# Neighbourhood attention on tokens ordered by columns, 208 keys to a half, with the probabilities as the standing operand; and two edits to the order of banks and of the sums of squares

## The chip, the cores and the metric

The kernel runs on one core of a Trainium2 chip. The time is device microseconds of that core, the median of three runs. The core's engines work side by side, each through its own list of instructions in order, and wait for one another on semaphores: TensorE (PE, with its weight loads as PEld), VectorE (DVE), ScalarE (ACT), GpSimd (POOL) and SyncE (SP), which here issues most of the DMAs. PE writes to eight banks of PSUM.

## The reference, cut to what matters

A block of two token mixers and an MLP, then two more layers, on 16 meta tokens and 256 tokens laid out on a grid of 4 rows by 64 columns, width 1024, all in float32. The part that the change rewrites is the neighbourhood attention (8 heads of 64):

```
q, k, v = split(rms_norm(h) @ w_in)                 # h: 16 meta + 256 tokens
for each token at (row r, column c):
    window: all 4 rows, 16 columns from start = clip(c - 8, 0, 48)
    s_win  = q.k * 64**-0.5 + rpb[dr + 7, clip(dc, -15, 15) + 15]   # -1e30 outside the window
    s_meta = q.k_meta * 64**-0.5
    p = softmax(concat(s_win, s_meta))
    o = p_win @ v_win + p_meta @ v_meta
```

A token of columns 0 to 31 never sees a column past 47, and one of columns 32 to 63 never one before 16. Other parts touched are sums of squares over 1024 channels, `rsqrt(mean(x * x))`, for three of the norms: the one ahead of the MLP, the final norm of the first block ("fin") and the norm of the gated linear attention's output ("go").

## The kernel before

Every weight matrix is streamed as units of 128 x 1024 floats (512 KB): SP loads a unit into one of 6 slots of `raw`, ACT rounds it to fp32r (`wh`), DVE takes the rest (`wl = raw - wh`), and PE multiplies three times, `Xh*wl`, `Xh*wh`, `Xl*wh`, with the activations split in the same way. A unit of 256 columns is 24 products, and one of 512 columns (a `rows` unit, where tokens stand as weights and come out as rows) is 6 products to a block of tokens. ACT runs 4 units ahead (`LEAD`), DVE 3 (`AHEAD`), and five buffers hold `wh` and `wl`.

All five engines run through the same list of stages (`Walk.tiles`, `Walk.rows`): after a unit each engine takes one or more `step()`s of a side program, a Python generator with a `yield` at each step, so that the side work of a stage (attention, recurrence, pooling) sits between units. `w.steps` says how many yields go with a unit. After the last unit of a tile an engine runs `leave`, which reads the bank, and a step. In `tiles` the step comes before `leave`, and in `rows` too. Banks 0 to 3 (`main`) are handed out in turn to the matrix products, 4 to 7 (`side`) to side work; `take` waits for the events that freed a bank, and for a group of tiles all banks are taken before its first product.

The first stages are k, q, v, zf, zb, qh (all of `w_in`). k and q are products with unnormed activations `XU`, scaled afterwards by the row `rsB` of 1/rms; v and all later ones use the normed `XA`, which the side program `scaled` makes during k. Attention is the side program from v on. One of its rounds `s` holds, for tokens 0 to 127 and 128 to 255 apart (`t`), the scores of head `s` (`bank<-kT,qT`, 272 keys), the turning of the probabilities of head `s-1` (`bank<-C,sP`, three transposes) and the product with V of head `s-2` (`bank<-PT,vN` and `bank<-PTm,vM`: V's 64 columns stand as weights and 256 queries stream). Between them DVE adds the bias and finds the maximum, ACT takes the exponential with its sum, DVE the reciprocal (`share`), POOL multiplies the probabilities by it (`sP<-sP,nm`), and ACT copies the turned ones. Ordinary float32 products, as these are, show as two instructions each in the trace; a transpose shows as one.

Sums of squares: ACT squares tile after tile, POOL adds those of tiles 1 to 5 to tile 0's, and PE multiplies what is left by a matrix of ones (`bank<-sq,C`), once for the sum of 0 to 5 and once each for 6 and 7.

Of the kernel before, what the change touches and what calls it, by code (L numbers as in the profile page):

```python
# [7 lines left out]
F32 = mybir.dt.float32  # L8
# [22 lines left out]
for _n, _w in [("ident", 128), ("ones", 128), ("negones", 128), ("neguc", 128), ("strict", 128), ("negsb", 128),  # L31
               ("m64", 64), ("negwin", 64), ("cinv", 64), ("tril", 128)]:
    CCOLS[_n] = (sum(w for _, w in CCOLS.values()), _w)
# [67 lines left out]
def flat(x):  # L101
# [12 lines left out]
          "attention_dve": ("most", "score", "score_grid", "share"),  # L114
# [113 lines left out]
class Walk:  # L228
# [40 lines left out]
    def rows(self, label, name, c0, c1, start, unit, leave):  # L269
        width = min(512, c1 - c0)  # L270
        kn = 1024 // width
        for col in range(c0, c1, width):
# [8 lines left out]
            self.step()  # L281
            leave(col - c0)
            self.left.add((label, col - c0))

# [33 lines left out]
def build(nc, ws, par, cst, msk, xt, biasd, late, bsd, wtd, crd, out):  # L318
# [4 lines left out]
    with ExitStack() as ctx:  # L323
# [54 lines left out]
        bias = sbt(pna, "bias", [128, 8, 384])  # L378
        qT = sbt(pna, "qT", [128, 4, 256])
        kT = sbt(pna, "kT", [128, 4, 272])  # L380
        vN = sbt(pna, "vN", [128, 2, 512])
        vM = sbt(pna, "vM", [16, 512])
        sP = [sbt(pna, f"sP{i}", [128, 272]) for i in range(4)]
        PT = [sbt(pna, f"PT{i}", [128, 2, 256]) for i in range(2)]
        PTm = [sbt(pna, f"PTm{i}", [16, 256]) for i in range(2)]
        nmr = [sbt(pna, f"nm{i}", [128, 3]) for i in range(4)]
# [18 lines left out]
        B1s = [sbt(ph2, f"B1{n}", [128, 2112], F32R) for n in "hl"]  # L405

# [65 lines left out]
        ALONE = ("k", "zf", "a", "qk", "glr")  # L472
# [29 lines left out]
        one = {n: sem("l_" + n) for n in ("cst", "par", "crow", "bias", "msk", "wT", "bS", "late", "out")}  # L502
# [47 lines left out]


# [16 lines left out]
        def sync_program(e):  # L568
            c.start("sp")
            e.dma_start(P[:, :], par).then_inc(one["par"], 16)  # L570
            for i in range(len(items)):
                for n in {0: (0,), 1: (1, 2), 2: (3,)}.get(i, ()):
                    e.dma_start(h[:, 2 * n:2 * n + 2, :], xt[:, 2 * n:2 * n + 2, :]).then_inc(x_sem[n], 16)
# [20 lines left out]
        def tensor_program(e):  # L594
# [105 lines left out]
            def t_rows(label, name, c0, c1, X, ready, freed, tokens):  # L700
# [5 lines left out]
                def unit(j, q, kn, width, col):  # L706
                    e.wait_ge(*low_at(j))
                    hi, lo = (x.rearrange("p (k n) -> p k n", n=width) for x in half(j))
                    for b, t in enumerate(tokens):
                        for k in range(kn):  # L710
                            for event in ready(q + k):
                                e.wait_ge(*at(*event))
                            last = q + k == 7
                            m = three(bk(label, col, b)[:, 0:width],
                                      (X[0][:, q + k, t:t + 128], X[1][:, q + k, t:t + 128]),
# [56 lines left out]
            w.side.append(scaled(4))  # L772
            t_tiles("k", "w_in", 512, 1024, (XUh, XUl), unnormed("mix"), lambda t: [("kT", t)], n1=272)
            t_tiles("q", "w_in", 0, 512, (XUh, XUl), unnormed("mix"), lambda t: [("qT", t)], n0=16, n1=272)

            def attention():
                for s in range(10):
                    if s < 8:
                        po = 64 * (s % 2)
                        for t in range(2):  # L780
                            ps = side.take("qk", s, t)
                            e.wait_ge(*at("qT", s // 2))
                            e.wait_ge(*at("kT", s // 2))
                            e.matmul(ps[:, 0:272], qT[po:po + 64, s // 2, 128 * t:128 * t + 128],
                                     kT[po:po + 64, s // 2, :], start=True, stop=True).then_inc(*up("qk", (s, t)))
                            side.give(("qk", s, t), ("score", (s, t)))
                            yield
                    if 1 <= s <= 8:
                        for t in range(2):
                            ps = side.take("turn", s - 1, t)  # L790
                            S = sP[(2 * (s - 1) + t) % 4]
                            e.wait_ge(*at("prob", (s - 1, t)))
                            e.wait_ge(one["cst"], 16)
                            for r in range(2):
                                e.transpose(ps[:, 128 * r:128 * r + 128], S[:, 16 + 128 * r:144 + 128 * r],
# [1959 lines left out]
```

## Time and profile before

| | us |
|---|---|
| median of three runs | 880.95 (878.87 to 882.58) |
| the profiled execution | 878.87 |
| its span | 877.1 |
| PE busy | 843.7 |
| DVE busy | 631.2 |
| ACT busy | 492.1 |
| POOL busy | 112.1 |

The stretches of the program in the span: k and q from 8 to 37 us, v to 58, zf, zb and qh with attention to 128, the recurrence and the other products of `w_in` to 229, the mixing and the MLP to 456, then the second layer (with "fin" near 505) and the third (with "go" from 683 to 715).

A row of the timeline gives start and duration of an instruction or of a merged run of like ones. PE's instructions are pipelined, so that their durations overlap; what one costs is read from its start to the start of the next. In brackets stands how long the engine had been idle and who is inferred to have released it.

### The profile page before, as it was taken

What the parts mean: (1) busy time and instruction counts of PE and PEld (TensorE: products, weight loads), DVE (VectorE), ACT (ScalarE), POOL (GpSimd) and SP (SyncE); (2) the same over time, 40 slices, a digit from 0 to 9 for tenths busy, and PEclk for the clock granted to TensorE, in tenths of its full rate; (3) what the DMA queues carried; (4) which work ended last, traced back from release to release, by engine and by line L of the source; (5) the groups of instructions that cost most, each with busy time, mean ns of one, the idle gap of its engine ahead of it and who ended that gap; (6) DMA issues with size and microseconds to landing.
All of it is one profiled execution on the core that took longest, in us unless ns stands there. A gap on an engine that the chain in (4) does not pass through costs nothing.

```text
span 877.1 us, 16387 instructions
## 1 busy us (share of the span) xinstructions
PE 843.7 (96%) x6574; PEld 799.0 (91%) x6574; DVE 631.2 (72%) x1045; ACT 492.1 (56%) x884; POOL 112.1 (13%) x129
## 2 busy tenths in 40 slices
PE   5989989999999999999999899999999999999996
PEld 5967768998899999999999799999997999999995
DVE  6855636995699887878799776776788549455573
ACT  6544435775556747474666653554577457566541
POOL 0021227530102000000030420000202020000001
PEclk9999999999999999999999999999999999999999
DMA  9632334445458998989878445555656336545431
GB/s 359 243 106 68 97 97 129 128 149 150 116 195 273 317 354 303 364 295 367 277 246 286 162 149 181 172 193 193 192 158 191 108 96 198 187 144 155 144 112 48
DMA packets 47098, 168.93 MB, mean 193 GB/s; under 512 B 5168, under 2 KB 6320, under 8 KB 46896
## 3 DMA queue, kind: packets, MB, share of 16 engines
q1 hardware_dynamic: 46592, 165.34, 56.7%
q10 hardware_dynamic: 432, 2.56, 0.7%
q8 instruction: 52, 0.85, 0.4%
q14 instruction: 22, 0.18, 0.1%
HBM read 166.83 MB, written 1.05 MB: 191 GB/s over the span
## 4 chain that ended last, share of the span: by engine, by line
PE 82%; DVE 10%; ACT 4%; issue 2%; DMA 1%; POOL 1%; SPq 0%; POOLq 0%; DVEq 0%; ACTq 0%
PE bank L183 81%; DVE wl L222 4%; DVE raw L210 1%; ACT wh L192 1%; PE bank L186 1%; DMA raw<-in_ws 1%; DVE B1l L210 1%; DVE h L210 1%; ACT sq L189 1%; DVE B0l L222 0%; ACT B1h L189 0%; ACT L198 0%; DVE A L210 0%; ACT th L189 0%; POOL sq L222 0%
## 5 line engine op out<-in xcount | busy, mean ns | idle before, releaser
L222 DVE TENSOR_TENSOR wl<-raw,wh 128x1024 fp32r<-128x1024 f32 x259 | 323.8, 1262 | 19.7 <-ACT wh L192 19.0
L192 ACT CAST wh<-raw 128x1024 fp32r<-128x1024 f32 x259 | 269.2, 1047 | 111.4 <-PE bank L183 56.0
L183 PE MATMUL bank<-XAh,wl 128*128 128x256 f32 (+1 forms) x896 | 257.4, 287 | 5.1 <-DVE wl L222 4.5
L183 PE MATMUL bank<-XAh,wh 128*128 128x256 f32 (+1 forms) x896 | 251.2, 280 | 0.0
L183 PE MATMUL bank<-XAl,wh 128*128 128x256 f32 (+1 forms) x896 | 251.1, 280 | 0.0
L183 PEld LDWEIGHTS bank<-XAh,wl 128*128 128x128 f32 x896 | 170.5, 190 | 9.6 <-issue 6.3
L183 PEld LDWEIGHTS bank<-XAh,wh 128*128 128x128 f32 x896 | 170.8, 191 | 0.2
L183 PEld LDWEIGHTS bank<-XAl,wh 128*128 128x128 f32 x896 | 170.8, 191 | 0.0
L183 PE MATMUL bank<-B1h,wl 128*128 128x256 f32 (+1 forms) x464 | 130.2, 281 | 2.4 <-DVE B1l L210 2.4
L183 PE MATMUL bank<-B1h,wh 128*128 128x256 f32 (+1 forms) x464 | 129.0, 278 | 0.0
L183 PE MATMUL bank<-B1l,wh 128*128 128x256 f32 (+1 forms) x464 | 129.0, 278 | 0.0
L183 PE MATMUL bank<-B0h,wl 128*128 128x256 f32 (+1 forms) x392 | 110.8, 283 | 1.2 <-DVE B0l L222 1.2
L183 PE MATMUL bank<-B0h,wh 128*128 128x256 f32 (+1 forms) x392 | 109.3, 279 | 0.0
L183 PE MATMUL bank<-B0l,wh 128*128 128x256 f32 (+1 forms) x392 | 109.2, 279 | 0.0
L183 PEld LDWEIGHTS bank<-B1h,wl 128*128 128x128 f32 x464 | 87.2, 188 | 2.9 <-ACT B1h L189 2.8
L222 POOL TENSOR_TENSOR sq<-sq 128x256 f32<-128x256 f32 x25 | 29.7, 1187 | 470.5 <-ACT sq L189 468.9
L183 PEld LDWEIGHTS bank<-B1l,wh 128*128 128x128 f32 x464 | 87.6, 189 | 0.0
L183 PEld LDWEIGHTS bank<-B1h,wh 128*128 128x128 f32 x464 | 87.3, 188 | 0.1
L183 PEld LDWEIGHTS bank<-B0h,wl 128*128 128x128 f32 x392 | 73.9, 188 | 2.1 <-issue 2.0
L183 PEld LDWEIGHTS bank<-B0l,wh 128*128 128x128 f32 x392 | 74.0, 189 | 0.0
L183 PEld LDWEIGHTS bank<-B0h,wh 128*128 128x128 f32 x392 | 73.8, 188 | 0.1
L183 PE MATMUL bank<-wl,XAh 128*128 128x512 f32 (+1 forms) x176 | 62.9, 358 | 0.0
(247 smaller groups left out, 1219.3 us busy)
## 6 DMA issues: line engine op xcount, KB each, us to landing
raw<-in_ws SPq DMA_DIRECT2D x307, 512.0 KB, 4.5
bias<-in_bias ACTq DMA_DIRECT2D x1, 1536.0 KB, 9.4
h<-in_xt SPq DMA_DIRECT2D x4, 272.0 KB, 4.8
out<-h SPq DMA_DIRECT2D x4, 256.0 KB, 2.2
C<-in_cst SPq DMA_DIRECT2D x1, 544.0 KB, 7.7
crow<-in_crow ACTq DMA_DIRECT2D x1, 512.0 KB, 12.9
wT<-in_wt SPq DMA_DIRECT2D x1, 512.0 KB, 5.9
bS<-in_bs SPq DMA_DIRECT2D x1, 512.0 KB, 6.7
```

What stands on the lines that cost most here:

```text
L183: return self.real.matmul(*a, **k)
L186: return self.real.transpose(*a, **k)
L189: return self.real.activation(*a, **k)
L192: return self.real.copy(*a, **k)
L210: return self.real.scalar_tensor_tensor(*a, **k)
L222: return self.real.tensor_tensor(*a, **k)
```

## The change

**Order of the tokens.** A second copy of the input, `in_xk`, holds the 256 tokens by groups of eight columns, in each group row by row, with the 16 meta tokens in the middle: tokens 0 to 127 (columns 0 to 31), meta, tokens 128 to 255. It is loaded as `hK` in place of `h` at the start, and k, q and v are all made from it, unnormed; V's rows are scaled by `rcol`, the column of 1/rms, which three small products turn out of `rsK`. The keys of a half lie side by side: 208 of them for queries of columns 0 to 31 (128 tokens, 16 meta, 64 tokens), and 208 for the others. `in_xt` is loaded into `h` later, by ACT's queue, and `XA` is made during q instead of k; POOL puts `rsK` into the old order (`rsB`).

**Attention.** Both halves of a head go through one step. Scores are two products of 208 columns into one bank; bias and mask are added for 416 columns at once, meta keys included. The probabilities are turned without being divided first, by four transposes (keys 0 to 127 of one half, 128 to 255 of the other, and 112 keys around the meta tokens for each). They then stand as weights and V streams, 64 columns at a time: four products per head, out by queries. DVE divides the result of two heads (`oN`), two transposes per pair of heads turn it back, and ACT and DVE write it to `B0h` and `B0l` in the old order. POOL's multiplication is gone.

**Order of banks.** `Walk.rows` runs `leave` before the last step. Each tile of q takes a bank of its own.

**Sums.** All eight squares of the MLP's norm are added by POOL, and one product is taken, later. For "fin", ACT squares six tiles after the first half of the stage vn and two after the second, where it was four and four, and POOL adds tiles 1 to 5 after the first half. For "go", POOL adds the two squares of a head, and one product per head is left of two, one unit later.

```diff
@@ Walk.rows
                 if q + kn < 8:
                     self.step()
-            self.step()
             leave(col - c0)
             self.left.add((label, col - c0))
+            self.step()
...
-        ALONE = ("k", "zf", "a", "qk", "glr")
+        ALONE = ("k", "q", "zf", "a", "qk", "glr")
...
@@ tensor_program
-            w.side.append(scaled(4))
-            t_tiles("k", "w_in", 512, 1024, (XUh, XUl), unnormed("mix"), lambda t: [("kT", t)], n1=272)
-            t_tiles("q", "w_in", 0, 512, (XUh, XUl), unnormed("mix"), lambda t: [("qT", t)], n0=16, n1=272)
+            w.side.append(scaled(8))
+            XU = (XUh, XUl)
+            t_tiles("k", "w_in", 512, 1024, XU, unnormed("mix"), lambda t: [("kT", t)], n1=272)
+            t_tiles("q", "w_in", 0, 512, XU, unnormed("mix"), lambda t: [("qT", t)], n1=272)
...
+                        ps = side.take("scores", s)
+                        e.wait_ge(*at("qT", s // 2))
+                        e.wait_ge(*at("kT", s // 2))
+                        for b in range(2):
+                            m = e.matmul(ps[:, 208 * b:208 * b + 208], qT[po:po + 64, s // 2, b, :],
+                                         kT[po:po + 64, s // 2, 64 * b:64 * b + 208], start=True, stop=True)
+                        m.then_inc(*up("scores", s))
...
+                        e.transpose(ps[:, 0:128], S[:, 0:128], cst_("ident"))
+                        e.transpose(ps[:, 128:256], S[:, 288:416], cst_("ident"))
+                        e.transpose(ps[0:112, 256:384], S[:, 64:176], cst_("ident"))
+                        e.transpose(ps[0:112, 384:512], S[:, 208:320], cst_("ident")).then_inc(*up("turn", s - 1))
...
+                        for b in range(2):
+                            o = bk("pv", hh // 2)[:, 128 * b + 64 * (hh % 2):128 * b + 64 * (hh % 2) + 64]
+                            z = slice(0, 80) if b else slice(64, 112)
+                            e.matmul(o, PT[hh % 2][:, 128 * b:128 * b + 128], vN[:, b, vs], start=True, stop=False)
+                            m = e.matmul(o, PTm[hh % 2][z, 128 * b:128 * b + 128], vM[z, vs], start=False, stop=True)
+                        m.then_inc(*up("pv", hh))
...
+                        ps = side.take("na_turn", p)
+                        e.wait_ge(*at("out_nat", p))
+                        for b in range(2):
+                            m = e.transpose(ps[:, 128 * b:128 * b + 128], oN[p % 2][:, 128 * b:128 * b + 128],
+                                            cst_("ident"))
...
+            ps = side.take("rcol")
+            e.wait_ge(*at("rs", "mix"))
+            for b, t in enumerate((0, 144, 64)):
+                m = e.matmul(ps[:, 2 * b:2 * b + 2], rsK[:, t:t + 128], cst_("ident", 2), start=True, stop=True)
...
+            t_rows("v", "w_in", 1024, 1536, XU, unnormed("mix"), lambda b, col: [("v", (col, b))],
+                   ((0, 128), (144, 272), (64, 176)))
...
-            square_sums("mlp", ("o", 7), ("rs", "mlp"))
+            def mlp_sum():
+
+                if ("up0", 1) in w.left and sums:
+                    sums.clear()
+                    ps = side.take("sums", "mlp")
+                    e.wait_ge(*at("sq_add", ("mlp", 7)))
+                    e.matmul(ps[:, 0:256], cst_("ones"), sq_of("mlp", 0)[:, 0:256], start=True, stop=True).then_inc(
...
@@ scalar_program
             e.dma_start(bias[:, :, :], biasd).then_inc(one["bias"], 16)
+            e.dma_start(negw[:, :], negwd).then_inc(one["negw"], 16)
+            e.dma_start(h[:, :, :], xt).then_inc(one["h"], 16)
             e.dma_start(crow[:, :], crd).then_inc(one["crow"], 16)
...
-                for t in range(col // 128, col // 128 + 4):
+                for t in (6, 7) if col else range(6):
                     square("fin", t, ("h_down", t))
...
@@ vector_program
+                    e.wait_ge(*at("rs_nat", 0))
+                    e.wait_ge(one["h"], 16)
                     e.scalar_tensor_tensor(v[:, :], h[:, k, :], par_("norm_mix", k), rsB[:, :], ALU.mult,
...
+                        e.tensor_tensor(S[:, :], ps[:, 0:416], bias[:, s, :], ALU.add).then_inc(*up("score", s))
+                        e.wait_ge(*now("score"))
+                        e.tensor_reduce(nm[:, 0:2], S[:, :].rearrange("p (b n) -> p b n", b=2), AX.X, ALU.max,
...
@@ gpsimd_program
+                    a, b = (sq_of("go", (hh, v))[:, 0:256] for v in range(2))
+                    e.wait_ge(*at("go_sq", (hh, 1)))
+                    e.tensor_tensor(a, a, b, ALU.add).then_inc(*up("go_add", hh))
```

**What stands in a row on the engines.** First PE, in the stage zb, between two units (`XA*, w*`): before, the six transposes of a head's probabilities and its three products with V.

```order
L183 MATMUL bank<-XAl,wh 128x256
L186 MATMUL bank<-C,sP 128x128 x2
L186 MATMUL bank<-C,sP 16x128
L186 MATMUL bank<-C,sP 128x128 x2
L186 MATMUL bank<-C,sP 16x128
L183 MATMUL bank<-PT,vN 64x256 x2
L183 MATMUL bank<-PTm,vM 64x256
L183 MATMUL bank<-XAh,wl 128x256
```

And now: four transposes and four products of 64 columns.

```order
L183 MATMUL bank<-XAl,wh 128x256
L186 MATMUL bank<-C,sP 128x128 x2
L186 MATMUL bank<-C,sP 112x128 x2
L183 MATMUL bank<-vN,PT 128x64
L183 MATMUL bank<-vM,PTm 128x64
L183 MATMUL bank<-vN,PT 128x64
L183 MATMUL bank<-vM,PTm 128x64
L183 MATMUL bank<-XAh,wl 128x256
```

Second ACT, at the end of the stage v (`vM`, `vN`: the copies that free v's banks; `sP,nm`: the exponentials of a head). Before, the copies stand behind the exponentials.

```order
L192 CAST wh<-raw 128x1024
L189 ACTIVATE sP,nm<-sP,nm 128x272 x2
L192 COPY vM<-bank 16x512
L192 COPY vN<-bank 128x512 x2
L192 CAST wh<-raw 128x1024
```

Now they stand ahead of them, and the rows of V are scaled on the way.

```order
L192 CAST wh<-raw 128x1024
L195 ACTIVATE vN<-bank,rcol 128x512 x2
L195 ACTIVATE vM<-bank,rcol 112x512
L189 ACTIVATE sP,nm<-sP,nm 128x208 x2
L192 CAST wh<-raw 128x1024
```

Third DVE, between the scaling of k's second pair of tiles (`kT`) and that of q's (`qT`): before, all of `XAl<-vt,XAh` was over by then.

```order
L222 TENSOR_TENSOR kT<-bank,rsB 128x272 x2
L222 TENSOR_TENSOR wl<-raw,wh 128x1024 x2
L210 SCALAR_TENSOR_TENSOR qT<-bank,rsB 128x256 x2
L222 TENSOR_TENSOR wl<-raw,wh 128x1024 x2
L210 SCALAR_TENSOR_TENSOR qT<-bank,rsB 128x256 x2
```

Now the making of `XA` from `h` begins behind `kT`; these are the first rows of it (five more tiles of `vt` and six of `XAl` follow ahead of the second `qT`).

```order
L222 TENSOR_TENSOR kT<-bank,rsK 128x272 x2
L222 TENSOR_TENSOR wl<-raw,wh 128x1024
L210 SCALAR_TENSOR_TENSOR vt<-h,P,rsB 128x272 x2
L222 TENSOR_TENSOR XAl<-vt,XAh 128x272
L222 TENSOR_TENSOR wl<-raw,wh 128x1024
L210 SCALAR_TENSOR_TENSOR vt<-h,P,rsB 128x272
L222 TENSOR_TENSOR XAl<-vt,XAh 128x272
```


## Rows read from the trace of the kernel before

**Rows 1.** The page: busy engines, and the granted clock in 40 slices.

```profile
PE 843.7 (96%) x6574; PEld 799.0 (91%) x6574; DVE 631.2 (72%) x1045; ACT 492.1 (56%) x884; POOL 112.1 (13%) x129
...
PEclk9999999999999999999999999999999999999999
```

**Rows 2.** Waits of PE for POOL's multiplication: us in total, times, longest.

```profile
PE bank L186 <- POOL sP L219: 4.0, 3, 2.5
```

**Rows 3.** Timeline of PE and ACT at the end of v: start, duration.

```profile
57.31 1.18 PE L183 MATMUL bank<-kT,qT 64*128 64x272 f32 x4
...
61.49 0.37 PE L183 MATMUL bank<-XAh,wl 128*128 128x272 f32 x1 [3.00 <-DVE wl L222]
...
60.68 0.56 ACT L192 COPY vM<-bank 16x512 f32<-16x512 f32 x1
```

**Rows 4.** Timeline of PE, parts of attention between units.

```profile
66.12 0.82 PE L186 MATMUL bank<-C,sP 128*128 128x128 f32 x6
...
66.86 1.08 PE L183 MATMUL bank<-PT,vN 128*64 128x256 f32 x4
...
67.87 0.64 PE L183 MATMUL bank<-PTm,vM 16*64 16x256 f32 x2
...
68.44 0.39 PE L183 MATMUL bank<-XAh,wl 128*128 128x272 f32 x1
...
71.67 1.18 PE L183 MATMUL bank<-kT,qT 64*128 64x272 f32 x4
...
72.78 0.44 PE L186 MATMUL bank<-C,sP 128*128 128x128 f32 x2
```

**Rows 5.** Timeline of PE in the third layer: small products.

```profile
705.72 1.02 PE L183 MATMUL bank<-sq,C 128*128 128x256 f32 x4
...
706.67 0.45 PE L183 MATMUL bank<-gq,KI 128*64 128x64 f32 x8
...
706.95 0.40 PE L183 MATMUL bank<-gq,gk 128*64 128x64 f32 x4
...
707.28 0.66 PE L183 MATMUL bank<-gq,K 128*128 128x64 f32 x4
...
707.75 0.36 PE L183 MATMUL bank<-XAh,wl 128*128 128x256 f32 x1
...
711.88 0.37 PE L183 MATMUL bank<-XAh,wl 128*128 128x256 f32 x1
...
714.70 0.38 PE L183 MATMUL bank<-sq,C 128*128 128x256 f32 x1
```

**Rows 6.** Timeline of PE near 505 us; POOL's additions of squares.

```profile
505.29 0.45 PE L183 MATMUL bank<-sq,C 128*128 128x256 f32 x1 [3.58 <-POOL sq L222]
...
505.61 0.72 PE L183 MATMUL bank<-XAh,wl 128*128 128x256 f32 x1
...
510.14 1.02 PE L183 MATMUL bank<-sq,C 128*128 128x256 f32 x4
...
L222 POOL TENSOR_TENSOR sq<-sq 128x256 f32<-128x256 f32 x25 | 29.7, 1187 | 470.5 <-ACT sq L189 468.9
```

**Rows 7.** DVE after k; DMA: ACT's issue, its queue 20-22 us, landing.

```profile
13.51 0.42 ACTq L180 DMA_DIRECT2D bias<-in_bias  x1
...
26.64 0.50 DVE L210 SCALAR_TENSOR_TENSOR vt<-h,P,rsB 128x272 f32<-128x272 f32 x1
...
27.05 0.44 DVE L222 TENSOR_TENSOR XAl<-vt,XAh 128x272 fp32r<-128x272 f32 x1
...
28.75 0.78 DVE L222 TENSOR_TENSOR kT<-bank,rsB 128x272 f32<-128x272 f32 x2
...
29.45 2.35 DVE L222 TENSOR_TENSOR wl<-raw,wh 128x1024 fp32r<-128x1024 f32 x2
...
q10 hardware_dynamic: 52, 0.59, 70.3%
...
bias<-in_bias ACTq DMA_DIRECT2D x1, 1536.0 KB, 9.4
```

More of the change, by code:

```diff
@@ L501, in build @@
         x_sem = [sem(f"l_x{i}") for i in range(4)]
-        one = {n: sem("l_" + n) for n in ("cst", "par", "crow", "bias", "msk", "wT", "bS", "late", "out")}
+        one = {n: sem("l_" + n) for n in ("cst", "par", "crow", "bias", "negw", "h", "msk", "wT", "bS", "late", "out")}
         def landed(i):
@@ L776, in attention @@
             def attention():
-                for s in range(10):
+                for s in range(11):
                     if s < 8:
                         po = 64 * (s % 2)
[L780 to L787, printed above, removed]
-                    if 1 <= s <= 8:
[L789 to L795, printed above, removed]
-                                            cst_("ident"))
-                            e.transpose(ps[0:16, 256:384], S[:, 0:16], cst_("ident")).then_inc(
-                                *up("turn", (s - 1, t)))
-                            side.give(("turn", s - 1, t), ("turned", (s - 1, t)))
-                            yield
-                    if s >= 2:
@@ L1173, in square @@
                 if k == 7:
-                    squares.give(sq_at[site, 0], ("sums", (site, 5)))
+                    squares.give(sq_at[site, 0], ("sums", (site, 7 if site == "mlp" else 5)))
             def rsqrt(site, ps, N, after, rs=rsB):
@@ L1267, in meta_rows, with v_out @@
+            def v_out(col):
+                for b in range(3):
+                    e.wait_ge(*at("mm", ("v", 0, b)))
+                    n = 112 if b == 2 else 128
+                    e.mul(vM[:, :] if b == 2 else vN[:, b, :], bk("v", 0, b)[0:n, :], rcol[0:n, 2 * b:2 * b + 1]).then_inc(
+                        *up("v", (0, b)))
             def meta_rows(label, N, M):
@@ L1627, in gla @@
                     yield
-                    for v in range(2):
-                        squares.give(ns[v], ("go_sum", (hh, v)))
+                    squares.give(ns[0], ("go_sum", hh))
+                    squares.give(ns[1], ("go_add", hh))
                     yield
@@ L2577, in gpsimd_program @@
             w.side.append(pool_side())
-            w.rows("vn", "even_in", 2048, 3072, nothing, nothing, lambda col: squares("fin")(range(col // 128, col // 128 + 4)))
+            w.rows("vn", "even_in", 2048, 3072, nothing, nothing, lambda col: squares("fin")((6, 7) if col else range(6)))
             w.side.append(scaled(8))
```

321 lines of the change are left out of this document (175 added, 146 removed).

## The prediction

> **What bounds the kernel now.** I read the page first: PE is busy 843.7 of 877.1 us, at full clock in nearly all slices, while DVE has 72% and ACT 56% [rows 1]. So time can be had in two ways: products taken off PE, and PE's waits. The list of PE's waits and its timeline come next. In attention PE waits three times for POOL's multiplication of the probabilities, 4.0 us in all [rows 2]. At the end of v it waits 3.0 us more [rows 3]. The inferred releaser there is DVE's `wl`, but that is a unit prepared three ahead; what PE lacked was a bank. zf's second tile needs the bank that `vM` was read from, and ACT copies `vM` at 60.68 to 61.24, behind its exponentials; PE goes on at 61.49. [...] The longest wait, 3.58 us at 505.29, is for POOL's sum of squares, and the unit behind it takes 4.53 instead of 2.82 [rows 6], another 1.7.
>
> **Attention's products.** Now a head costs: two scores of 272 columns 72.78 - 71.67 = 1.11 us; six transposes 66.86 - 66.12 = 0.74; two products with V and the meta one 68.44 - 66.86 = 1.58 [rows 4]; together 3.43. Each product is two instructions, of about 0.25 with 256 columns.
> After: scores with 208 of 272 columns, 1.11 x 208/272 = 0.85. Four transposes at 0.74/6 = 0.123: 0.49. Turning back, two transposes to a pair of heads: 0.12 a head. The four products with V are eight instructions of 64 columns under 128 columns of weights. The trace has that form once: `gq,K`, four instructions in 707.75 - 707.28 = 0.47, or 0.118 each; with 64 columns of weights (`gq,KI`) eight take 706.95 - 706.67 = 0.28, 0.036 each [rows 5]. I take 0.118, since the form is the same: 0.94. Sum 2.40, so 1.03 less a head, **-8.2** for eight. The ends: 0.036 each would give -13; 0.25, as with 256 columns, would give 0.
> The row says that turning the operands round costs something: streaming 64 columns is not a quarter of streaming 256. [...]
>
> **What is added on PE.** q's 96 products stream 272 columns instead of 256: 2.82/24 = 0.118 each, times 16/256, times 96 = **+0.7**. `rcol`: three products of 2 columns, six instructions at 0.036 to 0.118: **+0.5**. v keeps its 72 products of 512 columns.
>
> **Waits that go.** The bank at the end of v: ACT now copies before its exponentials, and the copies wait only for v: **-3.0 and -1.6**, with the clock. If ACT were late with something else, this would stay; ahead of the copies it has only a rounding (`wh`) that runs 4 units ahead. POOL's multiplication: **-4.0**. What is late next there? From the scores to the turning lie now one addition, one maximum and two exponentials; the order gives them two units everywhere, but one unit, turned and V products for the last head, about 4.2 us against some 3 by the 0.39 to 0.56 us that instructions on such tiles take now [rows 3, 7]. I count nothing new. At 505 us POOL's five additions move ahead by most of a stage, and the squares of tiles 6 and 7 need no POOL: **-3.6 and -1.7**. DVE and ACT work during the wait, but `wl` of the next two units is made before it; so the time does not come back at once.
>
> **The sums.** For "go", two products a head cost 706.67 - 705.72 = 0.95 us; one costs about half, and at 505.29 one took 0.32 [rows 5, 6]. Four heads: -1.9. The last sum now waits for POOL's addition (1.19 us mean [rows 6]), and the earlier ones have a unit of cover: +0.5. **-1.4**. For the MLP three products become one, 0.32 each: **-0.6**.
>
> **Waits that come.** (1) Start of v. The four tiles of q now have a bank each, so v, which takes three banks at once, needs the scaling `qT` of q's third tile, the last but one thing that DVE does for q. And the making of `XA` lies in q now. From the end of k to that `qT`, DVE has in its queue: `kT` 0.7, four `wl` 4.7, eight pairs `vt` and `XAl` at 0.41 + 0.35 = 6.1 (start to start; 6.5 with waits for ACT between), three `qT` 1.1: 13.0 us [rows 7]. PE needs for q 4 x 3.0 + 0.5 = 12.5. So PE waits 0.5, 0.7 with the semaphore. Moreover `XA` needs `h`, the third load of ACT's queue, behind 1664 and 208 KB. k ends near 25.7 (q ends at 37 and has four units), and DVE asks for `h` some 2.0 later, at 27.7. The queue moved 0.59 MB in 2 us between 20 and 22 us; `bias`, issued at 13.5, landed after 9.4 [rows 7], so at 22.9, and by this rate began at 17.6. At the same rate 2960 KB end at 27.8; at the mean rate of `bias` from its issue, 163 KB/us, at 31.6. I take 28.3, nearer to the first since weights ask for little at that time, and everything behind `h` in DVE's queue is late by as much: +0.6. Together **+1.3**; ends 0 and +4.6.
> (2) The last turning back stands right behind the last product with V, with DVE's division (some 0.4, like `kT` [rows 7]) between: **+0.8** with both semaphores.
> (3) The load of 1.3 MB more at the start takes some 4 us of DMA. SP's weights are ahead by six slots, so it is hidden; if not, see the rivals.
>
> **Sum.** -8.2 + 0.7 + 0.5 - 4.6 - 4.0 - 5.3 - 1.4 - 0.6 + 1.3 + 0.8 = -20.8. For small waits that I don't see in attention, where every engine is rearranged, +1. The profiled execution took 878.87 (span 877.1), and would take 859.1. The median before was 2.1 above it: **861.2 us**.
>
> **Rivals.**
> A. `h` comes late. [...] Then v starts 4.6 late instead of 1.3, and with 3 us of wait the low clock of rows 3 comes too, 1.6: 866. [...]
> B. The removed waits come back. PE reaches the same places 10 us earlier, with DVE, which is not faster, behind it; "fin" has ACT's copies of vn behind two roundings that wait for DVE. If half of the 13.9 us of waits and clock return: 868.
> C. The standing probabilities cost as much as the streamed ones: 8.2 less gained, 869.
> D. Slower. The mechanism is the clock. Where PE waited 3 us, a whole unit ran at half speed, at +1.7 us. Attention puts many short products between the units, more than now, with a wait of its own at the start of v. If the granted clock fell there and did not come back between the inserts, each of the 20 units from v on would lose 2.8; from the eighth on the 20.8 are gone, and with 12 it would be 895. Against it: waits of up to 2.5 us [rows 2] cost no clock that the page shows [rows 1]. [...]
> E. The edits don't do what they say: the last head's turning waits like before, or the bank at the end of v is still held. That is part of B.
>
> **How the numbers follow.** Forecast 0.68, A 0.12, B 0.10, C 0.05, D 0.02, and 0.03 for two of A to C at once (near 876). The forecast's own range: the V products from 0.05 to 0.15 give -4 to +2, the start of v -1 to +3, the small waits -1 to +3: 855 to 867. The range for all takes in A, B and C: **854 to 870**. A change under 0.5% (4.4 us, 876.5 to 885.4) can't be told from none here. Faster by more 0.95, within 0.03, slower 0.02.
>
> **What would show it.** In the profile after: a head's inserts on PE near 2.4 us and `vN,PT` near 0.12 each; no wait over 1 us between v and zf and no half-clock unit there; none near 490 to 500 us at the sum of squares; a wait of PE at the start of v, for `qT`, near 1.3, with DVE's first `vt` idle for `h` less than 1 us; POOL out of attention. I am wrong if PE's busy time falls by less than 8, or if waits of attention stay above 3 us.

## The result, and the profile after

The changed kernel took 875.44 us in the median of 11 runs (869.96 to 877.56), the kernel before beside it 879.73 (878.87 to 886.15): a ratio of 0.993, with a 95% interval of 0.9903 to 0.9956. It is faster by 0.7%, and the forecast of 861.2 us, with its range of 854 to 870, is missed by 14 us. The profiled execution took 876.36 us, with a span of 874.6; 859.1 had been forecast for it.

The page of the changed kernel, busy engines, against [rows 1]:

```profile
PE 842.2 (96%) x6576; PEld 805.6 (92%) x6576; DVE 628.8 (72%) x1009; ACT 489.0 (56%) x869; POOL 102.0 (12%) x122
```

PE's busy time fell by 1.5 us, where the text had named 8 as the least. The waits of PE, changed kernel (in total, times, longest), answer to [rows 2]:

```profile
PE bank L183 <- DVE wl L222: 9.5, 3, 8.2
PE bank L183 <- issue: 3.9, 1, 3.9
PE bank L183 <- DVE B1l L210: 3.0, 2, 2.6
PE bank L183 <- DVE qT L210: 2.5, 1, 2.5
...
PE bank L186 <- DVE oN L222: 1.0, 2, 0.5
PE bank L183 <- DVE oN L222: 0.6, 1, 0.6
```

POOL is gone from attention, and three waits stand that the forecast had small or not at all: for `B1l`, for `qT` and the one put down to `issue`. (The 8.2 us for `wl` are the start of the program, 8.0 before.) Timeline of PE, changed kernel: the start of v, the end of v (where [rows 3] had 3.00), and one head of attention against [rows 4]:

```profile
41.53 0.47 PE L183 MATMUL bank<-wl,XUh 128*128 128x512 f32 x1 [2.52 <-DVE qT L210]
...
62.62 0.97 PE L183 MATMUL bank<-kT,qT 64*128 64x208 f32 x4
63.52 0.39 PE L183 MATMUL bank<-XAh,wl 128*128 128x272 f32 x1
...
66.66 0.60 PE L186 MATMUL bank<-C,sP 128*128 128x128 f32 x4
67.09 0.33 PE L183 MATMUL bank<-vN,PT 128*128 128x64 f32 x2
67.36 0.43 PE L183 MATMUL bank<-vM,PTm 48*128 48x64 f32 x2
67.72 0.43 PE L183 MATMUL bank<-vN,PT 128*128 128x64 f32 x2
67.99 0.39 PE L183 MATMUL bank<-vM,PTm 80*128 80x64 f32 x2
68.19 0.37 PE L183 MATMUL bank<-XAh,wl 128*128 128x272 f32 x1
```

From these starts the scores take 63.52 - 62.62 = 0.90 us (0.85 forecast), the four transposes 0.43 (0.49), and the eight instructions with V 68.19 - 67.09 = 1.10 (0.94). The bank at the end of v is free: no wait.

The two kernels side by side, by when PE reaches the same work:

| PE reaches | before | after | gained so far |
|---|---|---|---|
| first `q_,Xl` behind attention | 145.23 | 135.35 | 9.9 |
| first `B1h,wl` of the MLP | 273.47 | 264.51 | 9.0 |
| first product of tile a (258 columns) | 450.63 | 449.79 | **0.8** |
| first `gq` of the third layer | 679.69 | 677.91 | 1.8 |
| first `sq,sk` | 758.77 | 755.87 | 2.9 |

The MLP stage, in which the change touches one ones-product, eats 8 us. The waits there explain little of it: the one at `B1h,wl` is 2.64 us where the kernel before has 1.39. Products and granted clock of PE in 90 us of that stage, first before, then after (window, us, busy and count, PEclk, DMA share, GB/s):

```profile
310.00:400.00 90.00, 90.00 (x797) 1.00 0.90 325
```

```profile
310.00:400.00 90.00, 90.00 (x767) 1.00 0.87 314
```

Both are busy all the time, both at the full clock, and one does 30 products fewer: 112.9 ns a product before, 117.3 after. The groups of that window in the changed kernel (count, busy us, mean ns), PE and its weight loads:

```profile
L183 PE MATMUL bank<-B1h,wl 128*128 128x256 f32 x128 | 36.0, 281 | 0.0
...
L183 PEld LDWEIGHTS bank<-B1h,wl 128*128 128x128 f32 x128 | 24.6, 192 | 0.0
L183 PEld LDWEIGHTS bank<-B1h,wh 128*128 128x128 f32 x128 | 24.0, 188 | 0.0
L183 PEld LDWEIGHTS bank<-B1l,wh 128*128 128x128 f32 x128 | 24.0, 188 | 0.0
```

In the kernel before all three loads have 188 ns and the products 276. So the stream has two cadences; I call them short (113 ns from start to start) and long (118). The 1488 products from 282.10 us in the kernel before keep the short one to the end, the 1464 from 277.48 us in the changed one the long one; but in the 191 products without a break from 733.88 us in the changed kernel the short cadence turns into the long at 747.4 us, where the rows of `wl,XAh` begin. Counted in units of 24 over the whole timeline, the kernel before had about 1560 products in the long cadence and the changed one about 3600. At 4.4 ns each, the difference between the cadences, that is 6.9 and 15.8 us more than the short one.

The wait put down to `issue`, 3.9 us, stands where vn is first used. Timeline of DVE and PE, changed kernel:

```profile
514.79 1.41 DVE L219 TENSOR_SCALAR vn<-vn,ss 128x1024 f32<-128x1024 f32 x2
...
516.29 0.89 PE L183 MATMUL bank<-wT,vn 128*128 128x128 f32 x4 [3.94 <-issue]
```

The same product of PE in the kernel before, which the forecast had not looked at:

```profile
519.59 0.68 PE L183 MATMUL bank<-wT,vn 128*128 128x128 f32 x4 [0.25 <-issue]
```

The fin sum itself, 3.58 us in [rows 6], no longer waits. PE waits 0.25 us for the product with vn in the kernel before and 3.94 in the changed one: the wait moved there.

### The profile page after: what moved, and what is told of

Read it like the earlier page. It is cut to its first block, busy times and chain, and to the rows that moved or that the text cites. A ratio compares the mean times of both kernels' runs of the same rounds, so it can differ in the third digit from the quotient of the medians.

```text
span 874.6 us, 16326 instructions
## 1 busy us (share of the span) xinstructions
PE 842.2 (96%) x6576; PEld 805.6 (92%) x6576; DVE 628.8 (72%) x1009; ACT 489.0 (56%) x869; POOL 102.0 (12%) x122
## 4 chain that ended last, share of the span: by engine, by line
PE 79%; DVE 11%; ACT 4%; issue 3%; DMA 2%; SPq 0%; POOL 0%; POOLq 0%; DVEq 0%; ACTq 0%
PE bank L183 79%; DVE wl L222 4%; DMA h<-in_xt 2%; DVE raw L210 1%; DMA raw<-in_ws 1%; ACT wh L192 1%; DVE B1l L210 1%; DVE h L210 1%; DVE XAl L222 0%; ACT B1h L189 0%; DVE B0l L222 0%; ACT L198 0%; DVE A L210 0%; ACT sq L189 0%; PE bank L186 0%
## 5 line engine op out<-in xcount | busy, mean ns | idle before, releaser
L222 POOL TENSOR_TENSOR sq<-sq 128x256 f32<-128x256 f32 x31 | 34.6, 1116 | 504.0 <-ACT sq L189 502.1
L210 DVE SCALAR_TENSOR_TENSOR raw<-raw,crow 128x1024 f32<-128x1024 f32 x48 | 60.1, 1253 | 0.0
## 6 DMA issues: line engine op xcount, KB each, us to landing
h<-in_xt ACTq DMA_DIRECT2D x1, 1088.0 KB, 15.1
```

The costliest lines, as they stand in the source:

```text
L210: return self.real.scalar_tensor_tensor(*a, **k)
L222: return self.real.tensor_tensor(*a, **k)
```

## The experiments

Each was timed beside the kernel before. The changed kernel is "changed" below.

**two_sums**: the ones-product ahead of the MLP's stream issued twice.

```
+ e.matmul(ps[:, 0:256], cst_("ones"), sq_of("mlp", 0)[:, 0:256], start=True, stop=True)
  e.matmul(ps[:, 0:256], cst_("ones"), sq_of("mlp", 0)[:, 0:256], start=True, stop=True).then_inc(...)
```

> The changed kernel, with the one ones-product of the mlp square sum issued twice into the same place (the second overwrites the first; nothing else is touched). In the changed kernel's profile the 1464 products of the mlp stretch (277 to 450 us) start 117.5 ns apart; in the kernel before, where two ones-products stood ahead of the stretch, they start 113.3 ns apart, with the same granted clock of 1.00 in both. Theory 1, the stream of products has two cadences and the short products just ahead of a stretch pick one: with two products the stretch runs at 113.3 ns, 1464 x 4.2 ns = 6.1 us less, +0.25 us for the second product, so about -5.9 us (875.4 to 869.5 us in the median). Theory 2, the stretch is slower because of the weights' loads and casts or by the luck of one execution: the profile again shows a mixture or 117.5 ns, the time changes by +0.25 us (875.4 to 875.7).

The profile has the short cadence in all of the stretch (797 products in the window above). The times are 869.33 to 879.03, median 873.21, ratio 0.9915 (0.9884 to 0.9947): 2.2 us better than the first timing of changed, in the direction of theory 1, but spread over what both theories allow. The profile supports it, the median does not settle it. This profile took 873.21 us, between the two groups of times that appear further down. Its MLP stage is 5.9 us shorter than that of changed, but from tile a to the first `gq` it takes 230.1 us, 2 us longer.

**norm_early**: `vn` normed one pair of `ga` tiles earlier on DVE.

```
- if ts[0] == 2:      # norm vn behind the second pair of ga tiles
+ if ts[0] == 0:
```

> The changed kernel, with the two multiplications that make vn for the sgu products (vn_norm, 2 x 0.7 us on VectorE) done after the first pair of ga tiles instead of the second. In the changed kernel TensorE waits 3.94 us at 516.29 for them, and the 24 products behind took 4.3 us instead of 2.8, at a lower clock. Theory 1, the wait that the prediction took away at 505 us stands here now, since the end of VectorE's chain and not the POOL square set the time in this stage: vn is ready some 2.7 us earlier (513.5 instead of 516.2), the wait falls to about 1 us and the clock stays up: -3 to -4.5 us, 871 to 872.5. Theory 2, the 1.4 us that VectorE now spends ahead of the low halves of the next weights make those late and the wait goes over to the weights: 0 to -1 us. If the products of the mlp stretch change their cadence by themselves (113.3 or 117.5 ns), the time moves by another 6 us in some executions whatever the edit.

Median 873.35, ratio 0.9897 (0.9866 to 0.9928), about 0.3% under changed. PE, norm_early:

```profile
514.02 0.68 PE L183 MATMUL bank<-wT,vn 128*128 128x128 f32 x4 [0.94 <-issue]
515.11 0.38 PE L183 MATMUL bank<-XAh,wl 128*128 128x256 f32 x1 [0.41 <-DVE wl L222]
```

The 3.94 us became 0.94, with 0.41 for the weights. From the first product of tile a to the first `gq` it takes 674.71 - 450.56 = 224.2 us where changed takes 228.1 and the kernel before 229.1: theory 1, -4.0 us in the stage.

**h_first**: `h` loaded ahead of `bias`.

```
+ e.dma_start(h[:, :, :], xt)...
  e.dma_start(bias[:, :, :], biasd)...
  e.dma_start(negw[:, :], negwd)...
- e.dma_start(h[:, :, :], xt)...
```

> The changed kernel, with the load of h (1088 KB) issued ahead of bias and negw on ScalarE's queue instead of behind them. In the changed kernel h was there at 30.2 us, VectorE made vt and XAl out of it until 40.9 and only then the last qT, for which v's first bank waited 2.52 us (41.53), and the unit behind took 5.9 us instead of 4.4. Theory 1, the late h is the cause: it lands near 24 us, the last qT is done at about 38.5, the wait falls to 0 to 0.5 us and the clock stays up: -2.5 to -4 us, 871.5 to 873. Theory 2, bias now lands later than 45 us and the first scores wait for it, or the work on h meets the k tiles in the same queue and delays them as much: -1 to +1 us.

Median 872.45, ratio 0.989 (0.986 to 0.992). `h` lands 8.3 us after its issue instead of 15.1 (`bias` now 14.7 instead of 9.4), and PE waits 0.47 at the start of v. The first `q_,Xl` comes at 130.99 instead of 135.35: -4.4, theory 1. No wait for `bias` is in its list. From tile a to the first `gq` it takes 229.1 us, so 1 of the 4.4 us is lost again there.

**probe** and **probe2** (one execution each): short products behind single units.

```
+ sums.append(lambda: insert(mlp_list))   # behind a unit: 1 to 4 float32 ones-products, transposes, or fp32r products
```

> The changed kernel, with short products that nothing reads put behind single units (24 products) of the mlp stretch and of the stretch of gb, eo0 and eo1: 1, 2, 3 or 4 float32 ones-products of 256 or 64 columns, 1 or 2 transposes, 1 or 2 small fp32r products, in a written order. They add some 20 us of work in all, so its time is no comparison. Theory 1 (the short products pick the cadence of what follows): the cadence of the 24 products behind each one is 113 or 118 ns by the kind and count of what stood ahead, the same kind with the same answer, an odd count leaving 117.5 and an even one 113.3 or a toggle between them. Theory 2 (chance, or the loads): the cadences show no relation to the kinds, or one value throughout.

> The kernel probe again, with the same short products at the same places of the mlp stretch; in the stretch of gb, eo0 and eo1 other ones, a pair behind every unit: pairs that add up from two places (as a square sum does), pairs of 384 and 128 columns, two transposes. Its time is no comparison. If the cadence is picked by the kind and the place, the 50 stretches of the mlp part show the same sequence of 113 and 118 ns as in probe; if by chance or by how the stages before ran, they agree in no more than half of the places. In the other stretch: pairs of float32 products from 118 ns either go to 113 ns at once and stay there, which would make one such pair worth 720 x 4.2 ns = 3.0 us, or leave 118.

In the two stretches with inserts the cadence changed only where something stood between the units. (Elsewhere it also changed with nothing between, as at 747.4 us above; in mlp_old, at 716.13 us, there are 0.16 us between two starts instead of 0.11, and the cadence is long behind them.) Both kernels together, for the 24 or 48 products behind an insert:

| between the units | short stayed short | short to long | long to short | long stayed long |
|---|---|---|---|---|
| one float32 product, 256 columns | 0 | **12** | 6 | 9 |
| two of them | **13** | 0 | 6 | 11 |
| three of them | 0 | 4 | 3 | 1 |
| four of them | 0 | 3 | 4 | 0 |
| one float32 product, 64 columns | 3 | 0 | 2 | 6 |
| two of them | 0 | 5 | 4 | 0 |
| one transpose | 2 | 3 | 1 | 5 |
| two transposes | 0 | 3 | 4 | 6 |
| one or two small fp32r products | 8 | 0 | 1 | 9 |

So a single float32 product of 256 columns ended the short cadence in 12 of 12 places, a pair of that size in 0 of 13, and fp32r products left things as they were in 17 of 18 places. This is a matter of form and not of number alone: with 64 columns the single product ended it in 0 of 3 places and the pair did in 5 of 5 places, and four products of 256 columns did in 3 of 3. From the long cadence, one and two products of 256 columns led out in 6 of 15 and 6 of 17 places; four of them, and two of 64 columns, in 4 of 4 each. A rule of odd and even is out, and so is theory 2, that there is no relation. But the kind and the place don't fix it either: probe2 has the same inserts in the MLP part but for one more (three products, behind the eleventh), and 22 of the 52 units behind the shared inserts have the other cadence; behind the first single product probe went to short and probe2 stayed long. Chance or what ran before has a say.

**mlp_old** and **before_one**: the MLP sum of the kernel before put back into changed, and the changed sum put alone into the kernel before.

```
- sums.append(mlp_sum)                                  # before_one: the other way round
+ square_sums("mlp", ("o", 7), ("rs", "mlp"))
- if 1 <= t < (8 if site == "mlp" else 6):              # POOL adds squares
+ if 1 <= t < 6:
```

> The changed kernel with one part of the change undone: the mlp square sum is made again by three ones-products (squares 0 to 5 added up on POOL, 6 and 7 by themselves), as in the kernel before; all else as changed. By the prediction's sum this costs 0.6 us (+0.6 us, 876.0). By the cadence theory it stands two ones-products ahead of the 1464 products of the mlp stretch, which the two profiles with such a pair (before, and two_sums) ran at 113.3 ns and the three with one product at 117.5: -6.1 +0.6 = -5.5 us, 870 us in most executions, and its profile shows the weight loads of that stretch all at 188 ns and not one in three at 192.

> The kernel before with that part of the change alone: the mlp square sum by one ones-product of squares added up on POOL. By the prediction's sum -0.6 us (about 879.5). By the cadence theory the mlp stretch goes from 113.3 to 117.5 ns a product: 1488 x 4.2 ns = +6.2, so +5.5 us, about 885.5, and this part makes the kernel before slower by 0.6%.

mlp_old: median 870.91 (869.35 to 875.26), ratio 0.9897 (0.9868 to 0.9927). before_one: median 886.35 (884.48 to 887.62), **ratio 1.006 (1.0038 to 1.0082)**. This part of the change, taken alone, makes the kernel slower by 0.6%. The profiles have 797 products (mlp_old) and 767 (before_one) in the window above. Changed needs 449.79 - 264.51 = 185.3 us from the first MLP product to tile a, mlp_old 177.2; before 177.2, before_one 184.9. Of the 8.1 and 7.7, 1464 or 1488 products at some 4.4 ns are 6.4 and 6.5; most of the rest is the wait ahead of the stretch, in changed with a lower clock behind it (0.76 from 271.39 to 277.50 us, and 1.00 in mlp_old). Beside the kernel before the ratio of mlp_old is only 0.3% under that of changed, about 3 us, and the intervals overlap; before_one's interval lies wholly above 1. PE, changed and then mlp_old:

```profile
271.39 0.55 PE L183 MATMUL bank<-B1h,wl 128*128 128x256 f32 x1 [2.64 <-DVE B1l L210]
```

```profile
271.13 0.36 PE L183 MATMUL bank<-B1h,wl 128*128 128x256 f32 x1 [1.38 <-DVE B1l L210]
```

**fin_old**: the split of the fin squares undone (9 runs).

```
- for t in (6, 7) if col else range(6):
+ for t in range(col // 128, col // 128 + 4):
...          # and the same on POOL
```

> The changed kernel with the split of the fin squares undone: four squares behind each half of vn, as in the kernel before. The prediction gave this edit -3.6 us and -1.7 us of clock, so undoing it costs +5.3 us (880.7). The rival, seen in the changed kernel's trace: both waits stand ahead of the same product, the vn that VectorE norms, so that the wait of 3.58 us at the fin product only comes back in place of most of the 3.94 us at the sgu product, as in the kernel before, where the sgu product waited only 0.25: 0 to +1 us, 875.4 to 876.5, its profile with about 3.6 us at the fin product and under 1 us at the sgu product. The long mlp stretch may pick its cadence otherwise in an execution, 6 us, whatever the edit.

Median 875.75, ratio 0.9933 (0.9908 to 0.9959): the same as changed (0.993). PE, fin_old:

```profile
496.94 1.19 PE L183 MATMUL bank<-sq,C 128*128 128x256 f32 x2 [3.59 <-POOL sq L222]
...
512.31 0.68 PE L183 MATMUL bank<-wT,vn 128*128 128x128 f32 x4 [0.26 <-issue]
```

The rival holds, to within the spread. By the profiles the stage of the two waits is 2 us longer (230.2 against 228.1), which the medians do not show; two_sums, whose fin squares are those of changed, has 230.1 too, so this is not put down to the split. And there is a surprise in this profile, an execution of 870.84 us. PE in the MLP stage, fin_old:

```profile
310.00:400.00 90.00, 90.00 (x797) 1.00 0.90 334
```

It has the single ones-product ahead of the stretch, like changed, and the short cadence behind it; the 36 products before the single one were long here, so this is a step from long to short of the kind in the table.

**step_old**: in the row stages the side step again ahead of the hand-over of banks (12 runs).

```
+ self.step()
  leave(col - c0)
  self.left.add((label, col - c0))
- self.step()
```

> The changed kernel with one part undone: in the row stages the side step stands again ahead of the hand-over of the banks. The prediction gave this part -3.0 us of wait at the end of v and -1.6 us of clock. If that holds in the changed kernel too, the wait is back at the end of v (about 63 us): +3 to +4.6 us, 878.4 to 880. Rival: the new attention needs no bank there by that time, since q's banks are single now and the qT wait at the start of v has moved the units of v later: 0 to +1 us.

Median 880.06, ratio 0.9988 (0.9967 to 1.001), so +4.6 us against changed, with the wait back. PE, step_old:

```profile
66.35 0.56 PE L183 MATMUL bank<-XAh,wl 128*128 128x272 f32 x1 [2.97 <-issue]
```

**all3, pairs1, pairs2**: the first three repairs together; then with float32 pairs to lift two more long stretches.

```
+ pair()          # ahead of the i rows, and ahead of the gb tiles; pairs2: once more a unit later
```

> The changed kernel with the three repairs together: the ones-product of the mlp sum issued twice, vn normed one pair of ga tiles earlier, h loaded ahead of bias. If the three losses are separate: 875.4 - 5.9 (cadence) - 3 (wait for vn) - 3 (wait for qT) = 863.5, with a profile that shows none of the waits of 2.5 and 3.9 us and 113.3 ns in the mlp stretch. If they hide one another (the stretch behind takes up what the one ahead gives): no more than the best one alone gave against the kernel before, 0.989, about 869.5.

> The kernel all3 (863.3 us) with a pair of float32 ones-products that nothing reads, adding up from two places as a square sum does, at two more places: ahead of the i rows (118 us) and ahead of the gb tiles (525 us). In all3 the 24-product units between 132 and 192 us (408 products) and the 720 products behind 528 us run at 117.5 ns. The small products between the units of the first stretch are fp32r, which in probe never changed the cadence, so one pair ahead of it should hold for all. Theory 1 (a pair leaves 113.3 ns behind it): -1.7 and -3.0 us, +0.9 us for the pairs, so -3.8, about 859.5. Theory 2 (one pair does not lift a stretch that ran at 117.5 ns, as in one of the two cases that probe2 showed at its start): +0.9 us at most, 864.2, or one of the two stretches alone, 861 to 862.5.

> As pairs1, with a second such pair one unit later at both places. If a first pair sometimes fails and a second one lifts the stretch (probe2: 117.5 ns behind its first pair, 113.3 behind the next 7), both stretches run at 113.3 ns: -1.6 -2.9 +1.8 = -2.7 us against all3, about 860.6, below pairs1 only if pairs1 failed at the long stretch. If the cadence is not set by pairs: +1.8 us, 865.1.

all3: median 863.33, ratio 0.981 (0.9782 to 0.9837). Theory 1: its profile shows none of the waits at qT and vn, and 797 products in the window. The single repairs gave only 2.2, 2.1 and 3.0 us in the median, 7.3 together, where all3 gave 12.1; in their profiles they gave 5.9, 4.0 and 4.4 in the stages that they touch. The rest is probably the draw described below: 4 of the 5 times of all3 are in its lower group. The pairs failed: 864.99 and 864.54. The profile of pairs1 has both stretches long; that of pairs2 has the first long and 552 of the 720 products of the second short, which wins 2.4 us, no more than the pairs cost.

**after_again** (12 runs, nothing changed), **best** (three repairs, the sum of before instead of a doubled product) and **best_pair** (two products with different weights as the pair).

> The changed kernel, unaltered. If the cadence of the mlp stretch is drawn in every execution, its times fall again in two groups some 5 us apart (870 to 871.7 and 874.7 to 877.6), with fewer in the lower one, and a profile of the lower group would show 113.3 ns in that stretch. If the program fixes it, the spread is that of a single group, under 0.3%.

> The changed kernel with its losses mended and no product doubled: mlp sum by three ones-products as before, vn normed one pair of ga tiles earlier, h loaded first. From all3 (863.3): without the doubled product -0.25 us, and the wait at the start of the mlp stretch 1.4 us (as in mlp_old) where all3 had 2.64, so -1.2 +0.5 for the two more ones-products: 862 to 863 us in its lower group, 867 to 868 where the slow cadence is drawn. The forecast of 861.2 for the change would then be met within 0.2%, which says that these three are all that was missed. If they are not separate: 866 or more.

> The kernel best with one pair of products that nothing reads, with two different stationary matrices (384 and 128 columns, as in the last stage, where such a pair went from 117.7 to 113.3 ns in 24 of 24 places), ahead of the i rows and ahead of the gb tiles. If the form decides: both stretches at 113.3 ns, -4.7 + 1.0 = -3.7 us, 858.5 to 859.5. If it is where and when the pair comes that decides: +1.0 us, with one or both stretches still at 117.7 ns.

after_again: 871.76, 871.87, 872.03, and nine runs from 875.23 to 878.04; ratio 0.9937 (0.9911 to 0.9962). Two groups, as in the first timing (869.96, 871.03, 871.68, and eight from 874.68 to 877.56). best: 861.06, 861.59, 861.99, and 867.31, 867.67, 868.00, median 864.65, **ratio 0.9817 (0.9776 to 0.9857)**. best_pair: median 863.88, three runs from 860.68 and three from 866.13, ratio 0.9816, so no clear gain; its profile has the first stretch long and 576 of the 720 products of the second short. In best's profile (861.06 us) the MLP stage runs short, with 797 products in the window, and the wait at the start of v is small. PE, best:

```profile
38.28 0.47 PE L183 MATMUL bank<-wl,XUh 128*128 128x512 f32 x1 [0.48 <-DVE qT L210]
```

Most profiles fit the reading that the lower group has the short cadence in the MLP stage: 876.36 and 877.73 (changed), 881.97 (step_old) and 887.12 (before_one) have 767 products in the window, and 870.84 (fin_old), 869.35 (mlp_old), 863.23 (all3) and 861.06 (best) have 797. two_sums (873.21, 797) falls between. With a single product ahead of the stream the lower group has 3 of 11, 3 of 12 (changed), 3 of 9 (fin_old), 3 of 12 (step_old) and 0 of 7 runs (before_one), and norm_early and h_first have one low time of 6 each. With a pair or three ahead of it: 4 of 6 (mlp_old), 3 of 6 (best), 3 of 6 (best_pair), 4 of 5 (all3), 3 of 4 and 3 of 4 (pairs1, pairs2), and 52 of 72 of the kernel before, if the line is drawn at 882.5 us; there and in two_sums the times leave no gap between two groups. So it looks as if the program set the odds and the execution drew. No kernel was profiled in both of its groups, so this is inferred.

## Why the prediction was wrong

The profiled execution came out 17.3 us above the forecast for it (876.4 against 859.1). By the steps of the forecast:

- **The MLP sum, -0.6: wrong in sign, about +6.5 to +8.** The step "three products become one, 0.32 each" priced the products and not the stream behind them. before_one shows +6.5 us in the median, mlp_old -4.5 to -5.1 for putting it back (about -3 by the ratios), the profiles 7.7 and 8.1 in the stage. two_sums, where the doubled product is the only edit, has the short cadence back in its profile. This is the largest miss. No rival had it. The sign "PE's busy time falls by less than 8" did give it away: it fell by 1.5. Rival D spoke of PE's clock; the granted clock was 1.00 in both windows.
- **The fin wait, -3.6 and -1.7: the wait was hidden by the next one.** Undone (fin_old), it changed nothing in the median. The step "the time does not come back at once" looked at the next two units of weights and not at the product 14 us on, which needs vn. DVE norms vn behind the second pair of `ga` tiles, whose time hangs on PE, and on that chain the kernel before had only 0.25 us to spare. norm_early took 3.0 of the 3.94 us away, and with it the stage from tile a to the first `gq` is 4.9 us shorter than before, near the 5.3 that were booked. The 1.7 of clock moved with the wait: the mean granted clock is 0.62 from 505.61 to 510.14 us in the kernel before, and in the changed one 0.60 from 516.29 to 520.60 us. Rival B named the place, but had ACT's copies of vn in mind and half of the waits.
- **The start of v, +1.3: +4.0.** 2.52 us of wait and 1.5 of clock (18 products in 5.90 us where 4.38 is usual, at a mean granted clock of 0.71). `h` landed at 30.2, between the 27.8 and 31.6 worked out and 1.9 later than the value taken: behind `bias`, which landed near 23.6, the last 1296 KB took 6.6 us, 196 KB/us where some 290 had been taken. DVE's first `vt` was idle for `h` 2.06 us, where less than 1 was to be the sign. Rival A had named a late `h`, with 4.6 us of wait and 1.6 of clock; by what rule the queues share the DMA engines, no run shows. h_first: -4.4 us at the end of attention, -3.0 to -3.6 in the median. DVE, changed kernel:

```profile
30.27 0.92 DVE L210 SCALAR_TENSOR_TENSOR vt<-h,P,rsB 128x272 f32<-128x272 f32 x2 [2.06 <-DMA h<-in_xt]
```

- **The bank at the end of v, -3.0 and -1.6: right.** The 1.6 comes from rows: 24 products of 272 columns take 66.12 - 61.49 = 4.63 us [rows 3, 4], where 24 of 256 columns take 714.70 - 711.88 = 2.82 [rows 5], which would be 3.0 with 272. The granted clock of PE in the kernel before is 0.63 from 61.49 to 66.12 us, and 0.50 in the middle of it, from 63.00 to 64.50: part of the unit ran at half the clock, not the whole of it as in rival D. The wait is gone in the changed kernel, with a clock of 1.00 from 66.35 to 71.00 us; step_old brings 2.97 us of it back, with a clock of 0.50 in that window, and 4.1 to 4.6 in the median.
- **POOL's waits in attention, -4.0: right** in that they are gone; in their place PE waits three times for `oN`, 1.6 us in all, where +0.8 and part of the +1 had been set down. (The hand-overs by semaphore in the forecast, some 0.2 us each, were an estimate of mine; from the end of ACT's `vM` to PE's next product [rows 3] has 61.49 - 61.24 = 0.25 us.)
- **Attention's products, -8.2: near.** A head fell from 3.43 us to 0.90 + 0.43 + 1.10 and some 0.1 for its half of the turning back, 2.53, so -7.2. The eight instructions with V took 0.14 each, not 0.118.
- **The go sums, -1.4:** from the first `gq` to `sq,sk` 79.1 us became 78.0, -1.1.
- The cadence took more than the MLP: the 17 units of 24 products in the recurrence (146 to 205 us before) ran short before and long in all profiles of the changed kernel and of those made from it, 1.8 us. Between them stand fp32r products, which left the cadence alone in 17 of 18 places of the probes, so it probably came from attention's end. This is read from traces, and the three attempts to lift it (pairs1, pairs2, best_pair) failed.

By stages, from the two profiles (us, less is faster; the forecast's terms in the stage where they were to act):

| stage | forecast | measured | missed |
|---|---|---|---|
| start to the end of attention | -12.5 | -9.9 | 2.6 |
| to the first `B1h,wl` of the MLP | 0 | +0.9 | 0.9 |
| MLP, to tile a | -0.6 | +8.1 | 8.7 |
| tile a to the first `gq` (fin, vn) | -5.3 | -0.9 | 4.4 |
| `gq` to `sq,sk` | -1.4 | -1.1 | 0.3 |
| to the end | 0 | +0.4 | 0.4 |
| sum | -19.8 | -2.5 | 17.3 |

In the first row the start of v is 2.7 us over its term and attention's products 1.0 short; some 1 us came the other way, and where is open. Of the 8.7 in the MLP, 6.4 are the cadence and some 2 the longer wait with its clock. The other way round, best, which mends the first three and keeps the rest of the change, reaches 861 to 862 in its lower group, where the forecast stood at 861.2; half of its times are in the group near 868, and its median is 864.65. That the lower group meets the forecast is in part luck: best has another MLP sum than the change, and terms of either sign in the rest.

What stays open is what sets the cadence. Where the cadence is long, the weight load of `B1h,wl` takes 192 ns instead of 188, one load in three. Whether this is cause or effect no run tells. Two float32 products of 64 columns, or four of 256, led out of the long cadence in 4 of 4 places each in the probes; neither was tried at the head of a long stretch.

## What to carry to other kernels

When a change takes work off the busiest engine and the time does not follow, count that engine's instructions in a window of the same work in both traces, before looking for waits: 797 against 767 showed here in one row what no list of waits showed. Before a wait is booked as gained, look for the next thing that the same engine will ask of the one it waits for, and how much time that has to spare; 0.25 us means that the gain moves there. And where the times of one kernel fall in two groups, compare group with group, and time the part alone: before_one cost one kernel and settled the sign of the largest term.

## What the runs showed of the hardware

- The main stream of fp32r products of 128 x 256 ran in one of two cadences at a granted clock of 1.00, 113 ns (797 products from 310 to 400 us, kernel before) or 118 (767, changed kernel). One float32 product of 256 columns between two units ended the shorter in 12 of 12 places, two did in 0 of 13, four in 3 of 3, and one or two small fp32r products did in 0 of 8. With 64 columns it was the other way round: one in 0 of 3, two in 5 of 5.
- Over 1464 products this is 6.4 us of 875. The times of one and the same program fell in two groups, 6 of 23 runs of the changed kernel near 871 and 17 near 877; that these are the two cadences is inferred.
- A load of 1088 KB issued behind 1664 and 208 KB on the same queue landed 15.1 us after its issue (changed), and 8.3 us when issued ahead of them (h_first).
- Float32 products of 64 columns under 128 columns of weights took 0.14 us an instruction, two to a product (changed kernel, 67.09 to 68.19 us).
